# Hybrid decoder block: eight-product projections in blocks 0 to 2, and the gates' first phase ahead of the logits from block 3 on

## The reference

```python
h = rmsnorm(x, norm_g)
proj = h @ w_in
q_g, k_g, v_g, gk_lr, gate_g, u_p, gate_p, q_m, gate_m = jnp.split(proj, SPLIT_IDX, axis=-1)
gk = jax.nn.log_sigmoid(gk_lr @ w_gk_up + b_gk) / GLA_NORMALIZER
o_gla = rmsnorm(gla_chunked(q_g, k_g, v_g, gk), gla_norm_g) * silu(gate_g)
o_pool = (multiscale_pool(u_p) @ pool_w) * pool_scale * silu(gate_p)
o_mem = memory_attention(q_m, rmsnorm(mem, mem_norm_g), w_mem_kv) * silu(gate_m)
x = x + concat([o_gla, o_pool, o_mem]) @ w_out
return rmsnorm(x, final_g)
```

## Time and profile before

| what | value |
|---|---|
| median of 3 runs | 1517.89 us (1515.62 to 1519.02) |
| the profiled execution, its own time | 1517.89 us |
| its span | 1516.2 us |
| PE busy | 1399.8 us, 92% of the span |
| DVE, ACT, POOL busy | 56%, 51%, 27% |
| block 0 from its first projection to block 1 | 156.1 us |
| block 1, block 2, a later block | 105.5, 90.7, 84.6 us |
| after the last block's products | 39.0 us |

### The profile page before, as it was taken

One profiled execution on the slowest core, in us unless ns is written; L12 is line 12 of the kernel. 1 busy time (PEld: TensorE's weight loads), 2 busy tenths in 40 slices (PEclk: granted clock), 3 DMA queues, 4 the chain that ended last, 5 costly groups with the idle time before them and its releaser, 6 DMA issues.

```text
span 1516.2 us, 39117 instructions
## 1 busy us (share of the span) xinstructions
PE 1399.8 (92%) x16380; PEld 1063.2 (70%) x16380; DVE 847.5 (56%) x1628; ACT 775.0 (51%) x1432; POOL 403.6 (27%) x344
## 2 busy tenths in 40 slices
PE   2487669899999999999999999999999999999996
PEld 2485466686958687786958687786959686776852
DVE  7674645645565555645555555546545655555452
ACT  5656636445464645545454546445454546455441
POOL 6144502423222322323221323223231223223000
PEclk9698789999999999999999999999999999999998
DMA  6145375452617264553617173543617172543501
GB/s 273 56 182 228 134 250 196 182 209 98 244 64 281 96 245 146 194 197 125 244 59 285 70 273 118 216 175 140 251 41 294 56 291 99 223 168 153 210 29 70
DMA packets 70493, 260.03 MB, mean 172 GB/s; under 512 B 7632, under 2 KB 13008, under 8 KB 67408
## 3 DMA queue, kind: packets, MB, share of 16 engines
q1 hardware_dynamic: 69920, 257.54, 45.7%
q10 hardware_dynamic: 432, 0.28, 0.1%
HBM read 229.47 MB, written 28.31 MB: 170 GB/s over the span
## 4 chain that ended last, share of the span: by engine, by line
PE 73%; ACT 5%; DVE 1%; issue 1%; POOL 1%; DMA 1%; ACTq 0%; DVEq 0%; POOLq 0%
PE bank L525 31%; PE bank L504 29%; PE bank L708 2%; PE bank L732 2%; PE bank L740 2%; PE bank L746 2%; PE bank L795 1%; ACT arena L982 1%; PE bank L603 1%; ACT arena L1195 1%; ACT arena L883 1%; PE bank L719 1%; PE bank L754 1%; PE bank L692 1%; ACT arena L1198 1%
## 5 line engine op out<-in xcount | busy, mean ns | idle before, releaser
L504 PE MATMUL bank<-ring,arena 128*128 128x512 f16 x1536 | 344.7, 381 | 6.4 <-DVE arena L1368 6.4
L525 PE MATMUL bank<-arena,ring 128*128 128x128 f16 x5376 | 321.1, 221 | 15.9 <-ACT arena L952 10.7
L525 PEld LDWEIGHTS bank<-arena,ring 128*128 128x128 f16 x5376 | 309.5, 99 | 23.6 <-ACT arena L952 11.3
L525 PE MATMUL bank<-arena,wres 128*128 128x128 f16 x5376 | 319.8, 220 | 2.3 <-DVE arena L1379 1.0
L525 PEld LDWEIGHTS bank<-arena,wres 128*128 128x128 f16 x5376 | 307.5, 99 | 6.8 <-issue 2.7
L504 PEld LDWEIGHTS bank<-ring,arena 128*128 128x128 f16 x1536 | 147.9, 98 | 181.9 <-issue 16.3
L504 PE MATMUL bank<-wv,arena 128*128 128x512 f16 x768 | 171.1, 383 | 0.0
L1716 POOL TENSOR_TENSOR arena<-arena 128x1024 f32<-128x1024 f32 (+2 forms) x45 | 65.5, 1456 | 386.6 <-ACT arena L856 384.3
L504 PEld LDWEIGHTS bank<-wv,arena 128*128 128x128 f16 x768 | 75.8, 99 | 90.4 <-issue 3.3
L1282 DVE SCALAR_TENSOR_TENSOR arena<-bank,sca,arena 128x256 f32<-128x256 f32 x64 | 30.9, 484 | 164.9 <-ACT arena L952 164.9
L1379 DVE SCALAR_TENSOR_TENSOR arena<-bank,sca,arena 128x512 f32<-128x512 f32 x64 | 47.8, 748 | 112.8 <-DMA arena<-in_x 90.8
(11 more groups left out here) (197 smaller groups left out, 1998.0 us busy)
## 6 DMA issues: line engine op xcount, KB each, us to landing
ring<-out_parts SPq DMA_DIRECT2D x120, 512.0 KB, 5.4
ring<-gate_parts SPq DMA_DIRECT2D x105, 512.0 KB, 6.6
ring<-side_parts SPq DMA_DIRECT2D x105, 512.0 KB, 5.6
arena<-in_xt SPq DMA_DIRECT2D x16, 1024.0 KB, 5.9
arena<-in_x SPq DMA_DIRECT2D x32, 512.0 KB, 4.1
out<-arena SPq DMA_DIRECT2D x32, 512.0 KB, 2.6
arena<-in_w_out SPq DMA_DIRECT2D x16, 512.0 KB, 5.4
out_parts<-arena SPq DMA_DIRECT2D x8, 512.0 KB, 4.2
```

What stands on the lines that cost most here:

```text
L504: mm = nc.tensor.matmul(ap, lhs, rhs, start=k == 0 and n == 0, stop=(k, n) == last)
L525: mm = nc.tensor.matmul(ap, w[:, p, k, j * P:(j + 1) * P], x_part(r, b)[:, k, :], start=fresh and j == 0 and k == 0 and n == 0, stop=k == ...
```

## The change

Blocks 0, 1 and 2 compute the four groups as eight-block products: `whole` makes one row (256 columns) of a group with 2·8·3 = 48 matmuls of 256 columns, two rows a group, with no sums of x or of weights. Only four pieces of each group are split in block 0 (c = 0, 1, 5, 6 slots). ACT copies the first row of a group out of PSUM (`first_row`) and DVE the second (`second_row`). In block 0 the gates' four rows stand behind the memory scores (`first_gate`). The sixteen pieces made of sums (MADE) follow later: POOL sums GG's and PM's in block 1, UM's and QK's in block 2 from weights fetched again; ACT and DVE split them (`made_hi`, `made_lo`) and ACT issues the DMAs that write GG's and PM's to DRAM (`made_out`). Block 3 starts on PE only when all sixteen are there (`lo_c` at 32). The loop of the other engines starts at block 3.

From block 3 on, PE runs GG phase 0 ahead of the logits; its third product, which writes bank 3, waits for `lr_out`. ACT takes GG's early copies ahead of the softplus, and DVE takes `add_11` of QK ahead of the bias.

```diff
-LATER = {g: NPROD * n for g, n in TURN.items()}
+LATER = {g: 4 * n for g, n in TURN.items()}
+COMBINED = 16
+MADE = ((GG, 6), (GG, 2), (GG, 3), (GG, 4), (PM, 6), (PM, 2), (PM, 3), (PM, 4),
+        (UM, 2), (UM, 3), (UM, 4), (UM, 6), (QK, 2), (QK, 3), (QK, 4), (QK, 6))
...
             step(0, True, False, False)
             step(1, False, True, False)
-            with eng.Fori(2, NB - 1) as i:
+            step(2, False, False, False)
+            with eng.Fori(WHOLE, NB - 1) as i:
                 step(i, False, False, False)
...
-                    for n in range(STAGES, KT + STAGES):
+                    sp.wait_ge(lo_c, LATER[UM] + 4)
+                    sp.wait_ge(d_fold, 16)
+                    sp.dma_start(rp, w_p).then_inc(d_wp, 16)
+                    keep_parts(GG, gg_d)
+                    for n in range(STAGES, 2 * STAGES):
+                        tile_in(n)
...
+            def whole(i, g, row, b):
+
+                for j in range(2):
+                    ap = bank[b][:, j * TB:(j + 1) * TB]
+                    for k in range(KT):
+                        c, q = 2 * row + k // 4, 2 * (k // 4)
+                        if j == 0 and k % 4 == 0:
+                            if i == 0:
+                                pe.wait_ge(lo_c, LATER[g] + c + 1)
+                            if i == 2 and g in (GG, PM):
+                                pe.wait_ge(d_slot[WHOLE_SLOT[g][c]], 16 * loads("whole", i, WHOLE_SLOT[g][c]))
+                        for n, (p, r) in enumerate(((0, 0), (0, 1), (1, 0))):
+                            mm = nc.tensor.matmul(ap, whole_parts[g][c][:, p, k % 4, j * P:(j + 1) * P],
+                                                  xs[:, 0, r, q:q + 2, (k % 4) * P:(k % 4 + 1) * P],
...
+            def product(i, g, c, b, name):
...
                     s = GG_SLOT[c]
-                    pe.wait_ge(d_slot[s], 16 * (3 * (i - 1) + 1) if s < 6 else 16 * (2 * (i - 1) + 1))
+                    pe.wait_ge(d_slot[s], 16 * loads("gates", i, s))
+                    if c == 2:
+                        pe.wait_ge(lr_out, i + 1)
...
                 pe.wait_ge(rb_st, 2 * (i + 1))
+                if i == WHOLE:
+                    pe.wait_ge(lo_c, COMBINED + len(MADE))
                 if first:
...
+                if not is_whole(i):
+                    pe.wait_ge(mix_m, i)
+                    phase(i, GG, 0)
                 pe.wait_ge(lr_out, i + 1)
...
                 if first:
+                    whole(i, QK, 1, 1)
                     fold_pool()
-                    phase(i, QK, 1, first)
+                    pe.wait_ge(lo_wv, 2)
+                    pe.wait_ge(cp[QK], 4)
+                    values(0).then_inc(pe_v, 1)
...
                     pe.wait_ge(lo_vk, 5)
-                    phase(i, PM, 0, first)
-                    values(1).then_inc(pe_v, 1)
-                    phase(i, PM, 1, first)
-                else:
-                    pe.wait_ge(mix_m, i)
-                    phase(i, GG, 0, first)
-                    phase(i, QK, 1, first)
+                elif is_whole(i):
+                    whole(i, QK, 1, 1)
                     pe.wait_ge(o_st, 4 * i - 1)
                     mix_sum(i - 1)
-                    phase(i, GG, 1, first)
-                    phase(i, QK, 2, first)
-                    phase(i, GG, 2, first)
+                    pe.wait_ge(mix_m, i)
+                    whole(i, GG, 0, 2)
+                    whole(i, GG, 1, 3)
...
+                    whole(i, UM, 1, 5)
                     pe.wait_ge(m_st, 4 * i - 3)
                     if second:
                         pe.wait_ge(o_scaled, 1)
-                    phase(i, PM, 0, first)
-                    phase(i, UM, 1, first)
-                    phase(i, PM, 1, first)
-                    phase(i, UM, 2, first)
...
                     pe.wait_ge(ad[GG], 4 * (i + 1))
-                    if not late(first, second) and not last:
+                    if not second:
+                        rms_sum(i + 1)
+                    pe.wait_ge(ad[QK], 4 * (i + 1))
+                    values(0).then_inc(pe_v, 1)
...
@@ -758,21 +879,34 @@
                     if not first:
                         out_proj(i - 1, n, i)
 
+                def first_gate(n):
+                    if first:
+                        if n == 2:
+                            pe.wait_ge(cp[GG], 4)
+                        if n == 3:
+                            pe.wait_ge(ad[GG], 4)
...
+            def made_hi(n):
+
+                g, c = MADE[n]
+                act.wait_ge(cb_ok, SUMS_AHEAD[n])
+                act.wait_ge(lo_c, COMBINED + n)
+                if (g, c) == (UM, 6) or (g, c) == (QK, 6):
+                    act.wait_ge(pe_f[g], 3 * WHOLE)
+                nc.scalar.activation(place[n][:, 0, :, :], made_from(n), ACT.Copy, scale=sw[:, g:g + 1]).then_inc(hi_c, 1)
+
+            def made_out(n):
+
+                g, c = MADE[n]
+                act.wait_ge(lo_c, COMBINED + n + 1)
+                dram = (gg_d if g == GG else pm_d)[:, c, :].rearrange("p (r k c) -> p r k c", r=2, k=4)
+                for r in range(2):
+                    act.dma_start(dram[:, r, :, :], place[n][:, r, :, :]).then_inc(d_new if n else d_new0, 16)
+
+            def fetch(g):
+
+                if g == UM:
+                    act.wait_ge(d_new0, 32)
...
+
+            def first_row(i, g):
+
+                act.wait_ge(pe_f[g], 3 * i + 1)
+                nc.scalar.activation(whole_out[g][0], row_of(i, g, 0), ACT.Copy, scale=scale[g][0]).then_inc(cp[g], 4)
...
+                    values_w_hi()
+                    act.wait_ge(g_ready, 4)
+                    first_row(i, QK)
+                elif is_whole(i):
+                    if second:
+                        act.wait_ge(o_sq2, KT)
+                    act.wait_ge(qm_hi, 2 * i)
+                    act.wait_ge(qm_lo, 2 * i)
+                    first_row(i, QK)
                 else:
                     act.wait_ge(ad[UM], 4 * i)
-                    if second:
-                        act.wait_ge(o_sq2, KT)
-                early_copies(i, QK)
-                if first:
-                    sum_squares(GV, rv, d_wv)
+                    early_copies(i, QK)
+                    act.wait_ge(ad[PM], 4 * i)
+                    early_copies(i, GG)
                 act.wait_ge(z_ok, 2 * (i + 1))
...
-                    early_copies(i, GG)
                 if second:
                     out_hi(0)
                     out_hi(1)
+                    made_hi(0)
+                if is_third(i):
+                    fetch(UM)
                 act.wait_ge(b_ok, 2 * (i + 1))
...
+                        tile_square(k)
+                    weights_hi(PM, range(4))
+                elif is_whole(i):
+                    act.wait_ge(mix_m, i)
+                    first_row(i, GG)
+                    if second:
+                        made_out(0)
+                        out_hi(2)
+                        out_hi(3)
+                        made_hi(1)
+                        made_hi(2)
+                    else:
+                        mixed_hi(i - 1)
+                    act.wait_ge(halo_ok, i + 1)
+                    act.wait_ge(mix_p, i)
...
+                if second:
+                    made_hi(7)
+                if is_third(i):
+                    made_hi(12)
                 if not late(first, second) and not last:
                     x_plain(i + 1)
                 p_exp_of(2)
...
-                        tile_square(k)
+                if is_third(i):
+                    made_hi(15)
+                    act.wait_ge(lo_c, COMBINED + len(MADE))
...
+            def second_row(i, g):
+
+                dve.wait_ge(pe_f[g], 3 * i + 3)
+                dve.wait_ge(cp[g], 4 * i + 4)
+                nc.vector.tensor_scalar(whole_out[g][1], row_of(i, g, 1), scale[g][1], None, ALU.mult).then_inc(ad[g], 4)
...
-                    weights_lo(QK, (4, 5, 6))
-                    dve.wait_ge(g_ready, 4)
+                if not is_whole(i):
+                    dve.wait_ge(qm_hi, 2 * i)
                     add_11(i, QK)
                 dve.wait_ge(pe_logit, i + 1)
...
                 nc.vector.tensor_reduce(mmax[:, 1:2], mixed, AX.XY, ALU.max,
                                         apply_absolute_value=True).then_inc(mmax_ok, 1)
+                if is_third(i):
+                    made_lo(15)
...
-                    pool.wait_ge(lo_c, LATER[GG] + NPROD)
-                    combine(PM)
+                if second:
+                    pool.wait_ge(lo_c, COMBINED)
+                    combine(GG, range(4))
+                    combine(PM, range(4))
+                if is_third(i):
+                    pool.wait_ge(d_raw, 64)
+                    combine(UM, range(4))
                 if not late(first, second) and not last:
...
-                    nc.gpsimd.memset(sT, 0.0).then_inc(zeroed, 1)
-                    nc.gpsimd.memset(S[:, 0, :, :], 0.0).then_inc(s_carry, 1)
```

(6 more changed lines are left out.)

695 lines of the change are left out of this document (405 added, 290 removed).

## The result

The changed kernel takes 1525.17 us (median of 5 runs, 1523.83 to 1527.37), the one before 1517.89 us (also 5 runs, 1515.62 to 1519.02). The ratio is 1.0051 with a 95% interval of 1.0037 to 1.0066. The forecast was 1508.0 us and faster.

What follows compares the result with a forecast made beforehand. TensorE alone was taken to bound the later blocks, start-up idle time the first ones. From 1517.89 us, -34 (block 0), -7 (block 1), +12.5 (block 2), +18 (repeated blocks) and +1 (cold start) gave 1508 us; range 1490 to 1526.

Steps and rivals of the forecast that it cites:

- Block 0: Start-up: plain projections drop splits and sums, so block 1 starts at 147 instead of 180.8: -34 us, trusted within 8.
- The repeated block: Blocks 3 to 15: GG phase 1 waits 2.1 us for VectorE's add, +1.4 us a block, +18 us in all.
- The clock behind the repeated wait: Blocks 3 to 15: whether the 2.1 us gap also lowers TensorE's clock; nothing in the sum for it.
- The sum: Whole kernel: -34 - 7 + 12.5 + 18, and 1 for block 3's cold start, on 1517.89 us.
- the rival: Thirteen repeated blocks: the gap drops the clock in more than half, adding 18 to 24 us: 1530; chance 0.12.
- The row that settled the case in the forecast: Wait behind the last block: 1.5 us without a matmul still shows clock 1.00, taken against a clock loss.
- the sum had 1 and 1.4: Block 3: 1 us for a cold start, and 1.4 us for its wait ahead of GG phase 1.
- Block 1: Block 1: 88.3 us work, 5.7 idle, 1.5 cold clock, about 3 for the ends: 98.5 against 105.5, -7.
- The forecast's idle time: Block 1: ScalarE's copy for the transposes comes 64.7 us in, TensorE is ready at 59: 5.7 us idle.
- VectorE beside GpSimd: Blocks 1 and 2: sixteen POOL sums may each hold VectorE once; nothing in the sum, up to 5 us in range.
- Block 2: Block 2: late turned probabilities cost 5.3 us, block 3's wait for the last lo part 7.1: 103 against 90.7, +12.5.

Runs made afterwards that it cites:

- experiments 1 to 3: Changed kernel with the order of before from block 3: 1499.2 us; kernel before with the reorder alone: 1541.36; changed kernel with only 24 matmuls ahead of the logits: 1491.38.
- Experiment 4: Changed kernel with 34 matmuls whose result nobody reads put into TensorE's wait ahead of GG phase 1: 1516.76 us.
- Experiment 7: Changed kernel with 10 matmuls nobody reads in TensorE's wait ahead of GG phase 1, leaving 1.34 us empty: 1517.78 us, from one run.
- Experiment 9: Changed kernel with GpSimd's eight sums of block 1 cut from 1024 to 8 elements per partition: 1521.57 us.
- Experiment 12: Changed kernel with the output weights' parts 4 to 7 made earlier in block 1 on ScalarE and VectorE: 1521.37 us.
- experiment 14: Changed kernel, 24 matmuls ahead of logits, last sum early, second four GpSimd sums held, output weights' parts 4-7 earlier, first product's four loads issued first: 1475.47 us.
- Experiment 6: Changed kernel with the last of the sixteen pieces made of sums finished early in block 2 on ScalarE and VectorE: 1518.17 us.
- experiment 1: Changed kernel with the order of before from block 3 on, plain projections kept: 1499.2 us, ratio 0.9889.

## Why the prediction was wrong, step by step

- **Block 0.** Forecast: block 1 starts at 147. It started at 142.94: 4 us better, inside the 8 us of doubt.
- **The repeated block.** Forecast: +1.4 us from a wait of 2.1 behind VectorE's add. Measured +1.33 and 1.92, with the chain of 6.02 us as read from the earlier trace rows. Right, and experiments 1 to 3 confirm it by removing it.
- **The clock behind the repeated wait. The first of two steps that failed.** The sum put the clock at nothing because behind the last block a stretch of 1.5 us shows clock 1.00, and the rival wanted a drop in most blocks or none. It drops in about one of three: 4 x 1.63 = 6.5 us in blocks 4 to 14, and block 11 has 0.5 more from a single wait for the residual's add. Experiment 4 shows it by taking it away. Block 3 adds 5.7 us where the sum had 1 and 1.4: after its 7.07 us wait it needs 7.35 us to the end of its first phase where block 6 needs 4.58 (2.8 more), and behind its own 1.92 us wait it loses 1.33 and 1.63 once more. So the clock costs 10.9 us where the sum had 1. Term by term, blocks 3 to 15 cost 29 us, not 19. The row that settled the case in the forecast was no witness. Its 1.5 us lie inside a wait of 2.20 us, and the clock inside a wait does not tell what comes behind it: in block 6 too it is 1.00 in the wait and falls 0.9 us later. In the kernel before, what follows that row is two short matmuls and a second wait, of 6.39 us, in which the clock is 0.50:

```profile
1478.50 0.38 PE L562 MATMUL bank<-small,ones 128*128 128x1 f32 x2 [2.20 <-DVE small L1678]
```

```profile
1481.10:1485.00 3.90, 0.00 (x0) 0.00 (x0) 3.36 (x2) 1.64 (x1) 0.00 (x0) 0.50 0.33 134
```

  To which of the two waits that fall belongs, no row tells. What was known of a wait of 2.1 us was only that one of 2.62 us ends at clock 0.50 and those of 0.5 us in each block at 1.00, so a share of the drops belonged into the sum. Experiment 7 gives the missing point below: at 1.34 us no drop, in one execution.
- **Block 1. The second step that failed.** Forecast 98.5, measured 107.7: a miss nearly as large. The forecast had 88.3 us of work, 1.5 of cold clock, 5.7 of idle time and 3 for the ends. The trace has TensorE busy for 92.4 us, 8.7 of them at half clock, and idle for 15.4, which are the waits of 7.62 and 7.74. So 6.7 of the 9.2 us are idle time and 2.5 are clock. The forecast's idle time ended 64.7 us into the block, with a copy by ScalarE; the first wait in the trace ends 64.2 us in, with VectorE's lo part of the queries. The second wait is the one that the forecast lacks. Behind the two stand costs that were put at nothing. One is VectorE beside GpSimd. By the Trainium skill (SBUF — State Buffer, "Who interferes with whom"), named in the forecast, the loser of the shared port blocks fully. The traces agree: the scan 5.42 for 1.27, each of its halves 2.7 us, about as long as one of GpSimd's sums. The forecast kept it out of the sum because VectorE is busy for less than 60% of the block; but what counts is the one operation on the chain, and that met a sum. Experiment 9 prices it at some 3.4 us. The other, the larger one, is the load of the stored output weights, 7.7 us of wait. The forecast counted ScalarE's queue and no transfer, although the block's whole shift brought those loads, 4 MB at 329 to 344 GB/s, into the open. Experiment 12 shortened the chain ahead of it, not this wait, and experiment 14 left the product at the same place of the block; that the wait comes of the loads' amount and the pace of the stores is argued from the full DMA engines and not shown.
- **Block 2.** Forecast 103, measured 104.15, and both waits are where they were placed: 5.6 us (forecast 5.3) for the turned probabilities and 7.07 us (forecast 7.1) for the last lo part. Experiment 6 removes the second.
- **The balance.** The forecast's 1508.4, less 4.1, plus 9.2, 1.2 and 10 gives 1524.7; measured 1525.2. By the same sum, either of the two misses alone would have left the kernel 2 to 3 us under the time before; together they turned the sign. The plain projections did bring 17 us (experiment 1), which the reorder more than spent.

## What to carry to other kernels

Work that is moved ahead of a wait should be about as much as the wait asks for: with 24 matmuls ahead of the logits the block got 0.7 us shorter than with none, with 72 it got 1.3 longer, since the logits feed a chain of 6 us whose cover had been those matmuls. A wait that is repeated is priced with the clock behind it, read from windows behind waits of known length and never inside them, and in shares if the known cases lie on both sides of its length. Where a stage gets shorter, look at what its length had hidden: a load, or another engine's work, that now falls beside the operation on the chain.

## What the runs showed of the hardware

The same wait of 1.92 us lowers the granted clock in 4 of the blocks 4 to 14 and leaves it in 7, each time for 3.4 us and from about 1 us behind the wait on, and the blocks where it does so mostly stand three apart. GpSimd's sums are themselves stretched when they meet VectorE's two-input operations, from 2.35 to 3.26 us. Putting them off cost 10 us: with both engines in use in that stretch, the meeting moved and did not go.
